# Two blocks of language-model work on one Trainium2 core: the expert stages put into one block, and the products of experts 34 to 127 widened to 512 columns

## The chip, the cores and the metric

One core of one Trainium2 chip runs the whole program. The metric is the device time of one execution in microseconds, as the median of several.

## The reference, cut to what matters

The reference runs a mixer block (attention with modulation) and then a second block on 256 tokens of width 2048, all in float32. The change lies in the last part of the second block, `peer_ffn`: 16384 small experts, of which each token and head picks 16.

```python
q = (xt @ wq).reshape(-1, PEER_HEADS, 2, PEER_HALF)          # 8 heads, 2 halves of 128
s = jnp.einsum('thpc,hpnc->thpn', q, keys)                   # 128 keys each
sv, si = lax.top_k(s, PEER_TOPK)                             # 16 best of each half
cand = (sv[:, :, 0, :, None] + sv[:, :, 1, None, :])...      # 256 sums
cid = (si[:, :, 0, :, None] * N_KEYS + si[:, :, 1, None, :])...
top_s, top_j = lax.top_k(cand, PEER_TOPK)
eid = jnp.take_along_axis(cid, top_j, axis=-1)
gate = jax.nn.softmax(top_s.astype(jnp.float32), axis=-1)
act = jax.nn.gelu(jnp.einsum('thkd,td->thk', ue, xt)...)     # ue = u[eid]
return jnp.einsum('thk,thkd->td', (gate * act).astype(xt.dtype), ve)   # ve = v[eid]
```

Then `h = layernorm(ALPHA * h + ff, ln2_g, ln2_b)`.

## The kernel before, in words

**Numbers.** Every float32 operand of a product is split into two float32r parts, hi (rounded by ScalarE) and lo (what is left, taken by VectorE). A product is three: hi hi, hi lo and lo hi, all added up in one PSUM bank (`mm3`, L159 to L164).

**Weights.** All weights go through one pipeline of slabs of 128 x 1024 values (512 KB), numbered through the whole program. SyncE loads them into four buffers `raw` (`load_slabs`, L131), ScalarE rounds halves of 512 columns into `w_hi` (`round_slab`, L146), VectorE subtracts into `w_lo` (`split_slab`, L153); both have two buffers. TensorE counts finished halves in `multiplied`, which lets ScalarE overwrite `w_hi`; `hi_ready`, `lo_ready` and `raw_ready` are the other counts.

**The expert part** computes all 16384 experts densely, 128 groups ("experts" in what follows: expert j is the row of 128 experts with first key j), and multiplies each activation with a gate that is zero where nobody picked it. It stands in three blocks, each of which ends with a barrier of all engines:

1. *Query stage* (L1612 to L1698). Transposes h, then for each of the 16 lists (8 heads, 2 halves) two slabs give a query (`query`), a small product with the keys its scores (`score`, L1641), and VectorE the 16 best (`rank`, with `top_step`). The end of the last ranking ends the block.
2. *Expert stage* (L1700 to L1863). TensorE: for expert j two slabs of `u`, 16 chunks of 128 features, three products of 256 columns (all tokens) per chunk, into bank j % 2 (`experts`, `feature_slab`). ScalarE: Gelu from PSUM into `wt[:, j, :]` (`activate`, L1752), in order with its rounding, two slabs ahead. VectorE: between the splits of the first 32 experts, for each head, the 16 best of 256 sums and the numbers of the picked experts. Then, beside experts 32 and 33, the softmax of all gates (Exp on ScalarE, L1765; the rest on VectorE, L1850 to L1853), which sets `g_ready`. GpSimd then adds the 8 x 16 x 2 columns of gates into a table in HBM, `g_dram`, by 256 indirect transfers (L1725), and waits after each head.
3. *Output stage* (L1866 to the end). GpSimd fetches the gate table, two experts at a time, through four buffers `pick` (L1891) and multiplies `wt` by them (L1896), as fast as it can, also the four last (L1912). ScalarE and VectorE split the gated weights of each expert (`wj_hi` L1922, `wj_lo` L1925) and the slabs of `v`; TensorE multiplies, 24 products of 512 columns per expert, and adds everything up in all 8 banks. A layernorm ends the program (L1963 on).

`acc_free` in stage 2 counts the banks that TensorE may write. The order on each engine is the order in which the code is written.

## Time and profile before

| what | value |
|---|---|
| time, median of 3 runs | 3189.55 us (3186.62 to 3190.53) |
| the profiled execution: its time, its span | 3186.14 us, 3184.5 us |
| granted TensorE clock, mean | 0.961 |
| TensorE, VectorE, ScalarE, GpSimd busy | 92%, 56%, 45%, 20% of the span |
| expert stage, first product to last | 1693.5 to 2432.2 us |
| output stage, first product to last | 2441.8 to 3159.6 us |
| HBM read, written | 532 MB, 21 MB: 174 GB/s |

Times on the axis of the trace count from the first instruction. "Busy" of TensorE counts overlapping products once; the length printed for one product (0.28 or 0.39 us) is its way through the array, and the pace of a full stream is the distance between starts. A bracket behind an instruction gives the idle time of its engine before it, and who ended it. In a group, busy us and the mean in ns of one stand behind the first bar, idle time before it behind the second.

### The profile page before, as it was taken

How to read it: one execution, taken by the hardware profiler on the slowest of the kernel's cores; microseconds unless marked ns; L12 is line 12 of the kernel's file. 1: busy time of each engine (PE TensorE's matmuls, PEld its weight loads, DVE VectorE, ACT ScalarE, POOL GpSimd, SP SyncE). 2: the span in 40 equal slices, each digit the busy share in tenths (PEclk: the TensorE clock that was granted, in tenths of full speed). 3: DMA queues.
4: the chain of work that ended last, by engine and by line, in shares of the span. 5: the costliest groups of instructions: out<-in, count | busy, mean ns of one | idle time of the engine just before them, and what ended most of it. 6: DMA issues, size and time to landing. Idle time of an engine off the chain costs nothing. (4 is left out here: it accounts for less than half of the span.)

```text
span 3184.5 us, 54921 instructions
## 1 busy us (share of the span) xinstructions
PE 2920.6 (92%) x17320; PEld 2551.2 (80%) x17320; DVE 1782.8 (56%) x3239; ACT 1423.2 (45%) x2600; POOL 626.3 (20%) x488
## 2 busy tenths in 40 slices
PE   6879997799989699987798999999998999999996
PEld 4658784688757599966698999999998778888885
DVE  5784325532355665446687874444445985555556
ACT  6663234422444344443344444444444445555553
POOL 0030001200000000010000028778775750000000
PEclk9999998799989799988899999999999999999998
DMA  6873237332425355534454567877777876666664
GB/s 237 288 229 127 87 111 278 93 122 96 139 85 180 99 182 188 165 126 134 162 167 154 181 185 181 182 184 180 183 184 243 278 237 193 193 192 192 194 193 132
DMA packets 182878, 554.10 MB, mean 174 GB/s; under 512 B 53664, under 2 KB 53696, under 8 KB 179488
## 3 DMA queue, kind: packets, MB, share of 16 engines
q1 hardware_dynamic: 137696, 517.03, 50.1%
q0 software_dynamic: 44544, 32.10, 6.2%
q10 hardware_dynamic: 576, 4.19, 0.3%
q8 instruction: 33, 0.54, 0.1%
q14 instruction: 29, 0.24, 0.0%
HBM read 532.13 MB, written 21.10 MB: 174 GB/s over the span
## 5 line engine op out<-in xcount | busy, mean ns | idle before, releaser
L153 DVE TENSOR_TENSOR w_lo<-raw,w_hi 128x512 fp32r<-128x512 f32 x1888 | 1319.0, 724 | 1175.8 <-ACT w_hi L146 1173.0
L146 ACT ACTIVATE w_hi<-raw 128x512 fp32r<-128x512 f32 x1888 | 1144.4, 629 | 989.9 <-PE PS L164 924.7
L162 PE MATMUL PS<-h_hi,w_hi 128*128 128x256 f32 x2944 | 833.9, 283 | 14.1 <-ACT L1753 8.6
L163 PE MATMUL PS<-h_lo,w_hi 128*128 128x256 f32 x2944 | 831.2, 282 | 0.0
L164 PE MATMUL PS<-h_hi,w_lo 128*128 128x256 f32 x2944 | 831.1, 282 | 0.0
L162 PEld LDWEIGHTS PS<-h_hi,w_hi 128*128 128x128 f32 x2944 | 564.7, 192 | 16.6 <-issue 10.9
L164 PEld LDWEIGHTS PS<-h_hi,w_lo 128*128 128x128 f32 x2944 | 564.8, 192 | 0.0
L163 PEld LDWEIGHTS PS<-h_lo,w_hi 128*128 128x128 f32 x2944 | 564.7, 192 | 0.0
L1725 POOL DMA_INDIRECT g_dram<-gt,spot x256 | 418.2, 1634 | 528.0 <-DVE gt L1853 417.9
L162 PE MATMUL PS<-w_hi,wj_hi 128*128 128x512 f32 x1024 | 402.8, 393 | 20.4 <-DVE wj_lo L1925 20.1
L164 PE MATMUL PS<-w_hi,wj_lo 128*128 128x512 f32 x1024 | 400.2, 391 | 0.0
L163 PE MATMUL PS<-w_lo,wj_hi 128*128 128x512 f32 x1024 | 400.1, 391 | 0.0
L162 PEld LDWEIGHTS PS<-w_hi,wj_hi 128*128 128x128 f32 x1024 | 193.2, 189 | 69.1 <-issue 15.2
L164 PEld LDWEIGHTS PS<-w_hi,wj_lo 128*128 128x128 f32 x1024 | 193.1, 189 | 40.6
L163 PEld LDWEIGHTS PS<-w_lo,wj_hi 128*128 128x128 f32 x1024 | 193.4, 189 | 39.8
L162 PE MATMUL PS<-x_hi,w_hi 128*128 128x256 f32 (+1 forms) x512 | 175.5, 343 | 12.1 <-ACTq L551 11.0
L1752 ACT ACTIVATE wt<-PS 128x256 f32 (+1 forms) x128 | 49.1, 384 | 298.1 <-PE PS L164 253.5
L163 PE MATMUL PS<-x_lo,w_hi 128*128 128x256 f32 (+1 forms) x512 | 174.2, 340 | 0.0
L164 PE MATMUL PS<-x_hi,w_lo 128*128 128x256 f32 (+1 forms) x512 | 174.1, 340 | 0.0
L162 PE MATMUL PS<-w_hi,x_hi 128*128 128x512 f32 x384 | 150.7, 392 | 1.3 <-DVE w_lo L153 1.3
L163 PE MATMUL PS<-w_lo,x_hi 128*128 128x512 f32 x384 | 150.3, 392 | 0.0
L164 PE MATMUL PS<-w_hi,x_lo 128*128 128x512 f32 x384 | 150.3, 391 | 0.0
(315 smaller groups left out, 2909.8 us busy)
## 6 DMA issues: line engine op xcount, KB each, us to landing
raw<-in_u_s SPq DMA_DIRECT2D x256, 512.0 KB
raw<-in_v SPq DMA_DIRECT2D x256, 512.0 KB
raw<-in_w_in_s SPq DMA_DIRECT2D x112, 512.0 KB
raw<-in_w_mod_s SPq DMA_DIRECT2D x96, 512.0 KB
raw<-in_w_in_a SPq DMA_DIRECT2D x64, 512.0 KB
raw<-in_w_in_b SPq DMA_DIRECT2D x64, 512.0 KB
raw<-in_w_out_s SPq DMA_DIRECT2D x64, 512.0 KB
g_dram<-h_buf SPq DMA_DIRECT2D x1, 16384.0 KB, 42.7
```

What stands on the lines that cost most here:

```text
L146: act.activation(w_hi[m % 2][:, half], raw[:, m % NRAW, half], ACT.Copy).then_inc(hi_ready, 1)
L153: dve.tensor_tensor(w_lo[m % 2][:, half], raw[:, m % NRAW, half], w_hi[m % 2][:, half].bitcast(F), ALU.subtract).then_inc(lo_ready, 1)
L162: pe.matmul(out, lhs[0], rhs[0], start=start, stop=False)
L163: pe.matmul(out, lhs[0], rhs[1], start=False, stop=False)
L164: return pe.matmul(out, lhs[1], rhs[0], start=False, stop=stop)
L1725: pool.indirect_dma_start(g_dram, bass.IndirectOffsetOnAxis(spot[:, t, n:n + 1], 0), gt[:, t, h, k:k + 1], None, compute_op=ALU.add).then_ ...
L1752: act.activation(wt[:, j if reg is None else reg + j, :], PS[:, j % 2, 0:T], ACT.Gelu).then_inc(acc_free, 1)
```

## The change

- The three blocks become one; nothing but counts of semaphores orders them.
- VectorE does the splits of the last two query lists inside `rank` also for slabs of `u`, and the picks of a head carry splits that lie four slabs further on. The picks run 5 heads, then `finish(0)` (softmax and places of heads 0 to 3), 3 heads, `finish(1)`.
- ScalarE does Exp in two batches (`gate_exp`), behind Gelu of expert 17 and of expert 33, and loads the Gelu table again at once. GpSimd starts to scatter heads 0 to 3 with the first batch.
- From expert 34 (`JW`) on, `h_hi` and `h_lo` lie side by side (`h_both`), and w_hi is multiplied with both in one product of 512 columns: hi hi lands in the lower half of the bank, hi lo in the upper half. w_lo times h_hi adds 256 columns to the lower half. ScalarE copies the upper half into `part`, VectorE adds the lower half (`add_low`), and ScalarE does Gelu from SBUF, one expert later.
- GpSimd fetches and weighs through two buffers (`GB` 2), four experts before the expert stage ends, and from then on at most eight experts ahead of TensorE.
- `wj_hi`, `wj_lo` lie over `si`, `spot` and `gt`; `part` lies in `pick`.

The core of the diff:

```diff
-        GB = 4
+        GB = 2
-        h_hi = buf3("h2_hi", [P, KT, T], R, hT)
-        h_lo = buf3("h2_lo", [P, KT, T], R, hT)
+        h_both = buf3("h2", [P, KT, 2, T], R, hT)
+        h_hi, h_lo = h_both[:, :, 0, :], h_both[:, :, 1, :]
...
+            part = pick[:, GB:2 * GB, :].rearrange("p a (b t) -> p (a b) t", b=2)
+            GH = HEADS // 2
+            J1 = HEADS * HEAD_SLABS // 2
+            JW = J1 + 2
...
+                    for h in range(HEADS):
+                        pool.wait_ge(g_ready, h // GH + 1)
...
+                    def weigh(reg, n):
+                        b = n // 2 % GB
+                        pool.wait_ge(gelued, max(JW, n + 2) if reg is None else reg + (n + 2))
+                        wait_multiplied(pool, None if reg is None else reg * 2, v0 + 2 * n - 16)
+                        pool.wait_ge(g_in[b], past(reg, 16 * (n // (2 * GB) + 1), 8 // GB))
+                        two = wt[:, n:n + 2, :] if reg is None else wt[:, ds(reg + n, 2), :]
+                        pool.tensor_tensor(two, two, pick[:, b, :].rearrange("p (j t) -> p j t", j=2), ALU.mult)\
+                            .then_inc(weighed, 2)
...
+                    pool.wait_ge(acc_free, JW + 2)
+                    for n in range(0, 2 * GB, 2):
+                        fetch(None, n)
+                    for n in range(0, 2 * GB, 2):
+                        weigh(None, n)
+                        pool.wait_ge(weighed, n + 2)
+                        fetch(None, n + 2 * GB)
+                    wait_multiplied(pool, None, v0)
...
+                    def experts_wide(reg, j):
+                        pe.wait_ge(acc_free, past(reg, j + 1))
...
+                                pe.matmul(PS[:, 6 + j % 2, :], w_hi[m % 2][:, c], h_both[:, kk, :, :].rearrange("p a t -> p (a t)"),
+                                          start=(kk == 0), stop=False)
+                                last = pe.matmul(PS[:, 6 + j % 2, 0:T], w_lo[m % 2][:, c], h_hi[:, kk, :],
+                                                 start=False, stop=(kk == KT - 1))
...
+                    def gate_exp(b):
+                        act.wait_ge(sh, GH * (b + 1))
+                        heads = slice(GH * b, GH * (b + 1))
+                        act.activation(gt[:, :, heads, :], gt[:, :, heads, :], ACT.Exp).then_inc(g_exp, 1)
+                        act.preload_act_table(ACT.Gelu)
...
+                    act.preload_act_table(ACT.Gelu)
+                    act.sem_inc(acc_free, 2)
+                    walk(0, J1 // 2 + 2)
+                    gate_exp(0)
+                    walk(J1 // 2 + 2, J1 + 2)
+                    gate_exp(1)
+                    def wide(reg, j):
+                        r2 = None if reg is None else reg * 2
+                        for s in range(2):
+                            round_slab(act, r2, m0 + 2 * j + s + 1)
+                        wait_multiplied(act, r2, m0 + 2 * j + 2)
+                        act.wait_ge(acc_free, past(reg, j + 1))
+                        act.activation(part[:, j % 2, :], PS[:, 6 + j % 2, T:2 * T], ACT.Copy).then_inc(low_out, 1)
+                    def gelu(reg, j):
+                        act.wait_ge(acc_free, past(reg, j + 3))
+                        act.activation(wt[:, past(reg, j), :], part[:, 2 + j % 2, :], ACT.Gelu).then_inc(gelued, 1)
+                    act.sem_inc(gelued, JW)
+                    act.wait_ge(g_ready, 2)
...
+                    with loop(act, N_KEYS - JW - 2, 2) as j:
+                        for u in range(2):
+                            wide(j, JW + 2 + u)
+                            gelu(j, JW + 1 + u)
...
+                    with loop(dve, GH + 1) as h:
+                        picks(h, 0)
+                    finish(0)
+                    with loop(dve, GH - 1) as h:
+                        picks(h, GH + 1)
+                    dve.wait_ge(tk, HEADS * per + 1)
+                    finish(1)
+                    def add_low(reg, j):
+                        dve.wait_ge(low_out, past(reg, j - JW + 1))
+                        dve.wait_ge(gelued, past(reg, j - 1))
+                        dve.tensor_tensor(part[:, 2 + j % 2, :], PS[:, 6 + j % 2, 0:T], part[:, j % 2, :], ALU.add).then_inc(acc_free, 1)
+                    with loop(dve, N_KEYS - JW, 2) as j:
+                        for u in range(2):
+                            for s in range(2):
+                                split_slab(dve, j * 2, m0 + 2 * (JW + u) + s + 1)
+                            add_low(j, JW + u)
```

Names of semaphores in the rows below are those under which they were allocated first: some carry the name of an earlier use of the same semaphore.

TensorE, from the query stage into the expert stage, before (the count it waits for at L172 is `acc_free`):

```order
L1641 MATMUL PS<-keys,qp 128x128 [waits s_free_5,acc_free_5]
L1641 MATMUL PS<-keys,qp 128x128
L64 UNCONDITIONAL_BRANCH
L1730 UNCONDITIONAL_BRANCH [waits barrier_Pool_Activation_PE_DVE_SP_release]
L34 UNCONDITIONAL_BRANCH
L34 ISA
L172 ISA [waits x_in0]
L162 MATMUL PS<-h_hi,w_hi 128x256 [waits lo_ready]
L163 MATMUL PS<-h_lo,w_hi 128x256
```

and TensorE at the start of the wide experts in the changed kernel (L1742 is the wait for a bank, L1745 the wide product, L1747 the narrow one; `h` is `h_both`):

```order
L164 MATMUL PS<-h,w_lo 128x256
L34 REGISTER_ALU
L34 COMPARE_AND_BRANCH
L34 UNCONDITIONAL_BRANCH
L34 ISA
L1742 ISA [waits x_in0]
L1745 MATMUL PS<-h,w_hi 128x512 [waits lo_ready]
L1747 MATMUL PS<-h,w_lo 128x256
```

The block's end before the experts is gone, and from expert 34 on two products stand where L162, L163 and L164 stood.

ScalarE around the softmax of the gates, before:

```order
L146 ACTIVATE w_hi<-raw 128x512 [waits multiplied,raw_ready1]
L146 ACTIVATE w_hi<-raw 128x512 [waits multiplied]
L146 ACTIVATE w_hi<-raw 128x512 [waits multiplied,raw_ready2]
L146 ACTIVATE w_hi<-raw 128x512 [waits multiplied]
L1765 ACT_TABLE_LOAD
L1765 ACTIVATE gt<-gt 128x256 [waits sh_u]
L1752 ACT_TABLE_LOAD
L1752 ACTIVATE wt<-PS 128x256 [waits multiplied]
```

and in the changed kernel at the second batch (L1813 is Gelu of a narrow expert, L1818 Exp, L1819 the load of the Gelu table, L1838 the copy of the upper half into `part`):

```order
L1813 ISA [waits multiplied]
L1813 ACTIVATE wt<-PS 128x256
L34 REGISTER_ALU
L34 COMPARE_AND_BRANCH
L1818 ACT_TABLE_LOAD
L1818 ACTIVATE gt<-gt 128x2x64 [waits sh_u]
L1819 ACT_TABLE_LOAD
L146 ACTIVATE w_hi<-raw 128x512 [waits multiplied,raw_ready1,g_ready_u]
L146 ACTIVATE w_hi<-raw 128x512 [waits multiplied]
L146 ACTIVATE w_hi<-raw 128x512 [waits multiplied,raw_ready2]
L146 ACTIVATE w_hi<-raw 128x512 [waits multiplied]
L1838 ACTIVATE pick<-PS 128x256 [waits x_in0,multiplied]
```

Two slabs were rounded ahead of Exp before; now Exp and both table loads stand ahead of the next rounding, which waits for `g_ready` too.

GpSimd, from the scatter to the weighing, before:

```order
L1725 DMA g_dram<-gt,spot 4194304x1 x31
L64 UNCONDITIONAL_BRANCH [waits scattered_u]
L1884 UNCONDITIONAL_BRANCH [waits barrier_Pool_Activation_PE_DVE_SP_gather]
L60 ISA x7
L1891 DMA pick<-g_dram 128x512 x4
L1901 DMA hb<-h_dram 128x4096 [waits h_stored]
L1903 DMA parc_12437<-in_ln_g 128x2048
L1903 DMA parc_12438<-in_ln_b 128x2048
L34 UNCONDITIONAL_BRANCH
L34 ISA
L1896 ISA [waits x_in2]
L1896 TENSOR_TENSOR wt<-wt,pick 128x512
```

and in the changed kernel (L1658 scatter, L1675 fetch, L1670 multiply, L1687 the load of h for the end):

```order
L1658 DMA g_dram<-gt,spot 4194304x1 [waits g_ready_u,scattered_u]
L1658 DMA g_dram<-gt,spot 4194304x1 x31
L1675 DMA pick<-g_dram 128x512 [waits x_in0,scattered_u]
L1675 DMA pick<-g_dram 128x512
L1670 TENSOR_TENSOR wt<-wt,pick 128x512 [waits multiplied,x_in1,normed]
L1675 DMA pick<-g_dram 128x512 [waits x_in3]
L1670 TENSOR_TENSOR wt<-wt,pick 128x512 [waits multiplied,x_in2,normed]
L1675 DMA pick<-g_dram 128x512 [waits x_in3]
L1687 DMA hb<-h_dram 128x4096 [waits h_stored,multiplied]
L1689 DMA parc_10498<-in_ln_g 128x2048
```

The block's end is gone, and each multiply waits for `multiplied`, the count of finished products, beside its fetch.

## Rows read from the trace of the kernel before

**Rows 1.** the page, section 1: busy time, share of the span and instructions of each engine

```profile
PE 2920.6 (92%) x17320; PEld 2551.2 (80%) x17320; DVE 1782.8 (56%) x3239; ACT 1423.2 (45%) x2600; POOL 626.3 (20%) x488
```

**Rows 2.** windows: length, busy us (instructions) of PE, PEld, DVE, ACT, POOL; PEclk, DMA share, GB/s

```profile
1600.00:1684.00 84.00, 84.00 (x707) 84.00 (x705) 73.22 (x302) 36.44 (x67) 0.00 (x0) 1.00 0.50 169
...
1900.00:2420.00 520.00, 520.00 (x4336) 520.00 (x4335) 233.69 (x361) 238.34 (x451) 406.85 (x250) 1.00 0.75 183
...
2470.00:2595.00 125.00, 116.75 (x494) 90.77 (x493) 113.68 (x104) 59.49 (x104) 92.11 (x97) 1.00 0.86 278
...
2640.00:3150.00 510.00, 510.00 (x2252) 422.30 (x2251) 291.49 (x470) 268.38 (x469) 0.00 (x0) 1.00 0.63 192
```

**Rows 3.** timeline of PE, query to expert stage: start, us, instruction, [idle before <-releaser]

```profile
1683.47 0.28 PE L164 MATMUL PS<-h_hi,w_lo 128*128 128x256 f32 x1
...
1693.53 0.57 PE L162 MATMUL PS<-h_hi,w_hi 128*128 128x256 f32 x1 [8.60 <-ACT L1753]
```

**Rows 4.** timeline of ACT at the same place

```profile
1683.79 0.38 ACT L1663 ACTIVATE qp<-PS 128x256 f32<-128x256 f32 x1 [2.25 <-PE PS L164]
1692.11 1.28 ACT L1753 ACT_TABLE_LOAD   x1 [7.94 <-PEq L64]
```

**Rows 5.** timeline of PE, expert stage to output stage

```profile
2432.06 0.28 PE L164 MATMUL PS<-h_hi,w_lo 128*128 128x256 f32 x1
2441.77 0.79 PE L162 MATMUL PS<-w_hi,wj_hi 128*128 128x512 f32 x1 [9.44 <-DVE wj_lo L1925]
2442.36 0.63 PE L163 MATMUL PS<-w_lo,wj_hi 128*128 128x512 f32 x1
2442.79 0.63 PE L164 MATMUL PS<-w_hi,wj_lo 128*128 128x512 f32 x1
```

**Rows 6.** timeline of ACT, expert stage to output stage

```profile
2440.73 0.42 ACT L1922 ACTIVATE wj_hi<-wt 128x256 fp32r x1 [7.87 <-POOL wt L1896]
```

**Rows 7.** timeline of DVE, expert stage to output stage

```profile
2441.29 0.42 DVE L1925 TENSOR_TENSOR wj_lo<-wt,wj_hi 128x256 fp32r<-128x256 f32 x1 [10.44 <-ACT wj_hi L1922]
```

**Rows 8.** timeline of PE, last matmul of the program

```profile
3159.41 0.39 PE L164 MATMUL PS<-w_hi,wj_lo 128*128 128x512 f32 x1
```

**Rows 9.** timeline of ACT where the gates get their exp

```profile
1882.95 1.28 ACT L1765 ACT_TABLE_LOAD   x1
1884.24 0.42 ACT L1765 ACTIVATE gt<-gt 128x256 f32<-128x256 f32 x1
```

**Rows 10.** timeline of DVE, softmax behind that exp

```profile
1884.69 0.42 DVE L1850 TENSOR_REDUCE gs<-gt 128x16 f32<-128x256 f32 x1 [1.04 <-ACT gt L1765]
...
1885.44 0.49 DVE L1853 TENSOR_TENSOR gt<-gt,gs 128x128 f32<-128x128 f32 x2
```

**Rows 11.** timeline of ACT, one expert of the expert stage

```profile
2300.00 0.38 ACT L1752 ACTIVATE wt<-PS 128x256 f32 x1 [2.35 <-PE PS L164]
2300.28 1.69 ACT L146 ACTIVATE w_hi<-raw 128x512 fp32r<-128x512 f32 x3
```

**Rows 12.** timeline of DVE, the same expert

```profile
2300.93 1.90 DVE L153 TENSOR_TENSOR w_lo<-raw,w_hi 128x512 fp32r<-128x512 f32 x3 [2.56 <-ACT w_hi L146]
```

**Rows 13.** the scatter of the gates, L1725: duration ns min/median/max, first and last start

```profile
L1725 POOL DMA_INDIRECT g_dram<-gt,spot x256: 1546/1551/2057, 1886.8 to 2413.6; - x128
```

**Rows 14.** groups by line, 2450 to 2590, while GpSimd weighs

```profile
L153 DVE TENSOR_TENSOR w_lo<-raw,w_hi 128x512 fp32r<-128x512 f32 x94 | 109.9, 1207 | 15.1 <-ACT w_hi L146 15.1
...
L1896 POOL TENSOR_TENSOR wt<-wt,pick 128x512 f32 x53 | 71.1, 1342 | 5.2 <-DMA pick<-g_dram 4.4
```

**Rows 15.** groups by line, 2640 to 3140, after it

```profile
L153 DVE TENSOR_TENSOR w_lo<-raw,w_hi 128x512 fp32r<-128x512 f32 x368 | 255.2, 693 | 214.5 <-ACT w_hi L146 214.5
```

**Rows 16.** timeline of PE near the end of the weighing

```profile
2603.01 0.49 PE L162 MATMUL PS<-w_hi,wj_hi 128*128 128x512 f32 x1 [2.43 <-DVE wj_lo L1925]
...
2604.59 0.63 PE L162 MATMUL PS<-w_hi,wj_hi 128*128 128x512 f32 x1
2605.02 0.63 PE L163 MATMUL PS<-w_lo,wj_hi 128*128 128x512 f32 x1
```

More of the change, by code:

```diff
@@ new lines, in _ @@
+                    wait_multiplied(pool, None, v0)
+                    pool.wait_ge(h_stored, 16)
+                    pool.dma_start(hb[:, :, :], h_dram).then_inc(late_in, 16)
+                    for i, name in enumerate(("ln2_g", "ln2_b")):
+                        pool.dma_start(par[i][:, :], bcast(io[name])).then_inc(late_in, 16)
+                    with loop(pool, N_KEYS - 4 * GB, 2 * GB) as j:
+                        for n in range(2 * GB, 4 * GB, 2):
+                            weigh(j, n)
+                            pool.wait_ge(weighed, j + (n + 2))
+                            fetch(j, n + 2 * GB)
@@ L1623, in _ @@
+                    for n in range(N_KEYS - 2 * GB, N_KEYS, 2):
+                        weigh(None, n)
                 @blk.tensor
@@ new lines, in _ @@
+                    expert_slab(None, v0, 0, 0, True, False)
+                    pe.wait_ge(acc_free, N_KEYS + 2)
+                    expert_slab(None, v0 + 1, 0, 1, True, False)
+                    for a in range(2):
+                        expert_slab(None, v0 + 2 + a, 1, a, False, False)
+                    with loop(pe, N_KEYS - 4, 2) as j:
+                        for u in range(2):
+                            for a in range(2):
+                                expert_slab(j, v0 + 4 + 2 * u + a, 2 + u, a, False, False)
@@ L1656, in _ @@
                     transposed_round(act, tr, h_hi, rnd, banks=(0, 1))
-                    act.sem_inc(acc_free, 2)
+                    act.sem_inc(q_free, 2)
                     with loop(act, 2 * HEADS, 2) as j:
@@ new lines, in _, with pair @@
+                    gelu(None, N_KEYS - 1)
+                    def pair(j, last):
+                        for u in range(2):
+                            split_weights(act, None, j, u)
+                            for s in range(2):
+                                if not (last and u == 1 and s == 1):
+                                    round_slab(act, None if j is None else j * 2, v0 + 2 * u + s + 1)
+                    with loop(act, N_KEYS - 2, 2) as j:
+                        pair(j, False)
@@ L1776, in _ @@
+                    dve.wait_ge(tk_q, 5 * 2 * HEADS + 1)
+                    step = chain(dve, "dve_last")
                     per = 10
```

382 lines of the change are left out of this document (154 added, 228 removed).

## The prediction

> **What bounds the kernel now.** First the page: TensorE is busy 92% of the span, VectorE 56%, ScalarE 45%, GpSimd 20% [rows 1], so most of the time can only be won by making TensorE's own stream shorter, and the rest by closing its holes. Then the windows by stage [rows 2], which tell where it is full. In the expert stage (1900 to 2420 us) PE is busy 520.00 of 520.00 us with 4336 products of 256 columns: 0.1199 us each, at granted clock 1.00, the 2.4 GHz level. An expert is 48 of them, 5.757 us. In the undisturbed output stage (2640 to 3150) it is full again: 2252 products of 512 columns in 510 us, 0.2265 us each, 24 to an expert, 5.436 us. Two 256-column products take 0.2398, so a 512-column one costs 0.0133 us less than two of 256.
>
> Between the full stretches are three holes. At the start of the expert stage the last query product begins at 1683.47, and the first expert product at 1693.53 [rows 3]: the rankings of VectorE have to end, then a block ends, then ScalarE loads a table at 1692.11 [rows 4]. At the start of the output stage the last expert product begins at 2432.06 and the first output product at 2441.77 [rows 5]: behind the block's end GpSimd must fetch and weigh before ScalarE can round the weights (2440.73) [rows 6] and VectorE take the rest (2441.29) [rows 7]. After both holes PE starts slowly, at the 1.2 GHz level: 0.43 us between 512-column products [rows 5], where 0.2265 is the rule. Third, while GpSimd weighs everything in one go (2470 to 2595), PE gets 494 products done where 125/0.2265 = 552 would fit, and VectorE is busy 113.68 of 125 us [rows 2]. The groups by line say why: w_lo<-raw,w_hi lasts 1207 ns there and 693 ns after it [rows 14, 15], beside a GpSimd multiply of 1342 ns, every 2.6 us.
>
> **The change, part by part.** All times are those of the one profiled execution (3186.14 us, span 3184.5), whose axis I carry on.
>
> *1. Query to expert stage.* No barrier is left: PE waits for acc_free, which ScalarE gives after the qp copy (1683.79) [rows 4], with its next instruction 0.28 later (as the copy at 2300.00 and its follower at 2300.28 [rows 11]), and one table load of 1.28. First expert product: 1683.79 + 0.28 + 1.28 + 0.15 for the signals = 1685.5, where it was 1693.53. That is 8.0 won. The old stage also took 2432.18 - 1693.53 = 738.65 us for 128 x 5.757 = 736.9; the 1.75 are the slow first products, and go, since PE now pauses 1.9 us with the score products in it. Against this, VectorE does its last two rankings and the first picks beside the first experts. In the query stage it is busy 73.22 of 84 us beside a full PE [rows 2], so it can just keep up; but the first split now waits for the table load, and the lag meets the first picks. I bound this stall by 0 and 3 us and take 1.5. Sum: 8.0 + 1.75 - 1.5 = **8.3 won**.
>
> *2. Gates in two batches.* Exp now stands behind the Gelu of expert 17 and of expert 33, with the next rounding behind it, where before two slabs had been rounded ahead of it. From the start of that Gelu: 0.28, Exp table 1.28 and Exp 0.4 [rows 9], Gelu table 1.28, then a half slab's rounding and, 0.65 after its start, its split of 0.69 [rows 11, 12]: 0.28 + 1.28 + 0.4 + 1.28 + 0.65 + 0.69 = 4.6 us. PE holds one prepared slab (24 x 0.1199 = 2.88), of which 0.3 has run. It waits 4.6 - 2.6 = 2.0 us. The second time ScalarE also waits for g_ready, 1.3 us of VectorE work behind Exp [rows 10], which the second table load covers. Twice 2.0: **4.0 lost** (0 if the tables did not have to change, 6 if VectorE is late as well). What it buys is an early scatter. It took from 1886.8 to 2413.6 [rows 13], 527 us; with the first batch ready near 1813 (expert 21 or 22), it ends near 2345, 60 us before the expert stage does. So fetching and weighing the first four experts costs nothing; without this lead it would be the old hole.
>
> *3. Wide products, experts 34 to 127.* Per k-chunk one 512-column and one 256-column product take the place of three: 0.2265 + 0.1199 = 0.3464 for 0.3597 us. 94 experts x 16 chunks x 0.0133 = **20.1 won**. The columns streamed are the same; what goes is the fixed part of one product in three. Above and below: the second product can't cost less than its columns do at 2.4 GHz, 0.1067, which would win 20 more; and the saving of a wide product over two narrow ones could be absent where two different weights alternate, which wins nothing. I take the row of the 512 products, where the weights also change each time. The added work is one more ScalarE activation of 0.38 and one VectorE add of about 0.42 per expert. ScalarE was busy 238 of 520 us, VectorE 234 [rows 2]. The order matters more: from the start S of the next expert, the copy starts at S+0.29, Gelu at S+0.57, rounding near S+0.92, the split ends at S+2.26, and PE wants it at S+2.77. The cover is 0.5 us, so this costs nothing; on VectorE the add lies in the gap before that split.
>
> *4. Expert to output stage.* GpSimd has weighed four experts by then. Left is the copy, Gelu of 126, the add, Gelu of 127 (start S+1.2), rounding of the weights at S+1.5, and from there to PE 2441.77 - 2440.73 = 1.04 [rows 5, 6]: 2.5 us, for 2441.77 - 2432.18 = 9.6. **7.1 won.** The fetches of h and the two parameter rows wait for the last expert product and have 690 us.
>
> *5. Weighing spread over the output stage.* The stage now lasts 3159.41 + 0.23 - 2441.77 = 717.9 us [rows 5, 8]; at full pace 128 x 5.436 = 695.8. GpSimd's multiply is now held to eight experts ahead of PE, one in 10.9 us in place of one in 2.6. A VectorE split held up for 1.3 us once in two experts has cover: a half slab is wanted 2.7 us and more after it could have been made. **22.1 won**, of which 13 are the lost products above and most of the rest the slow stretches. If each of 62 multiplies still cost what it costs now, 58 x 0.2265 / 49 = 0.27 us, 16.6 of it would stay; I take none, for the density is a quarter.
>
> *6. Clock.* A pause of 2.43 us near the end of the weighing was followed, from 2604.59, by eight products at 0.43 us [rows 16]. The pause at the switch to the output stage is nearest to it in length: I charge **1.7 lost** there, and nothing for the shorter ones.
>
> Sum: 8.3 - 4.0 + 20.1 + 7.1 + 22.1 - 1.7 = 51.9, from 3186.1 to 3134.2. The profiled execution lies 3.4 below the median of 3189.55; against the median it is 3137.7, rounded **3138 us**. Before the expert stage and behind the last product nothing changes.
>
> **Rivals.** *A, more is hidden than I see* (0.10): no stall at the gates or the start, cheaper narrow products: 5.5 and up to 10 more, 3123 to 3132. *B, the weighing still hurts* (0.08): VectorE held up by as much per multiply as now, 16.6, gives 3154. For it speaks only the 1207 ns. *C, the wide product saves nothing* (0.06): pace by columns alone, 3158. Against it stands the 0.0133 between the two full stages. The Trainium skill, page "TensorE: Matmul & The Clock Gate", section "Wait — 56ns, not 53.3ns?", has the fixed part of a product at about 2.5 ns when warm. By that rule part 3 wins 94 x 16 x 2.5 ns = 3.8 us as an estimate from the page, the sum is 3154, and the rows, with 13.3 ns, disagree.
>
> *D, slower* (0.04): the split comes late for every wide expert. ScalarE works in order, and the copy and one Gelu now stand ahead of the rounding. From a chain of 2.77 us on PE waits; from 0.55 us more per expert (51.9/94) all is lost. If Copy out of PSUM and Gelu out of SBUF had to change tables, 2 x 1.28, the chain is 4.8 and PE waits 2.05 x 94 = 193 us: 3331. Against it: Copy and Gelu alternate now, 0.28 apart, without a load [rows 11].
>
> **How the numbers follow.** My forecast has 0.72 (3132 to 3148, from the stalls at 0 to 6 and the clock at 0 to 7). The range must leave out at most 0.2: 3128 to 3156 cuts off half of A, C and D, 0.15 together. About 0.2% (6 us) is what can be told from no change. Faster 0.95, same 0.01, slower 0.04.
>
> **What would show it.** Right: wide experts 5.54 us apart with PE full; the first expert product near 1685.5; PE idle about 2 us behind L1819 twice; under 3 us before the first output product; the last scatter near 2345; w_lo near 700 to 800 ns in the output stage, and 5.44 us per expert from its beginning. Wrong: PE waiting for w_lo in the wide stretch (D), 5.7 us per wide expert (C), w_lo above 1000 ns with PE under full (B), the scatter ending behind the experts.

## The result, and the profile after

| kernel | median us | lowest to highest | ratio of the runs, 95% interval |
|---|---|---|---|
| before | 3190.04 (4 runs) | 3186.62 to 3191.83 | |
| changed | 3140.64 (4 runs) | 3137.06 to 3152.64 | 0.9853, 0.9825 to 0.9881 |

The change is 49.4 us faster, where 51.5 was forecast, and the median lies 2.6 us above the forecast of 3138. A second group of runs of the same two kernels (e1 below) has 3144.20 for 3190.49, 46.3 us; the median of all eleven executions of the changed kernel is 3142.5. The execution that was profiled took 3152.64 us (span 3150.9), 12 us more than the median of its group; the experiments below tell why.

The page of the changed kernel, section 1:

```profile
PE 2911.8 (92%) x15816; PEld 2475.9 (79%) x15816; DVE 1801.5 (57%) x3346; ACT 1450.7 (46%) x2697; POOL 621.6 (20%) x488
```

TensorE has 1504 products fewer than in [rows 1]: 94 x 16 chunks have two products in place of three. Its windows by stage (columns as in [rows 2]):

```profile
1600.00:1684.00 84.00, 84.00 (x706) 84.00 (x706) 72.59 (x298) 37.87 (x69) 0.00 (x0) 1.00 0.48 169
1900.00:2400.00 500.00, 500.00 (x2832) 433.51 (x2831) 266.09 (x442) 259.39 (x529) 353.85 (x224) 1.00 0.73 188
2450.00:2575.00 125.00, 125.00 (x553) 103.50 (x552) 79.18 (x116) 65.26 (x115) 22.31 (x24) 1.00 0.69 214
...
2640.00:3100.00 460.00, 460.00 (x2032) 380.87 (x2031) 289.21 (x424) 240.02 (x423) 73.25 (x78) 1.00 0.66 215
```

Two things stand here. In the output stage 553 products fit in 125 us, where 494 did [rows 2]: full pace from its beginning. And in the wide stretch PE is full, with 2832 products in 500 us, so a pair of them (one wide, one narrow) costs 0.3531 us, where 0.3464 was predicted.

The timeline of PE from query to expert stage answers to [rows 3]. Everything ahead runs 2.60 us later than in the profile of before (its last query product at 1686.07, there 1683.47):

```profile
1686.07 0.28 PE L164 MATMUL PS<-h,w_lo 128*128 128x256 f32 x1
1686.19 1.35 PE L1716 MATMUL PS<-keys,qp 128*128 x8
1688.21 0.38 PE L162 MATMUL PS<-h,w_hi 128*128 128x256 f32 x1 [0.68 <-ACT L1825]
```

From last query product to first expert product it is 2.14 us, for 10.06. ScalarE in front of the gates (a later stretch of its timeline) answers to [rows 9], and behind it stand the two first expert products that had to wait for the gates, on the timeline of PE:

```profile
1793.48 0.38 ACT L1813 ACTIVATE wt<-PS 128x256 f32 x1 [2.35 <-PE PS L164]
1793.88 1.28 ACT L1818 ACT_TABLE_LOAD   x1
1795.17 0.31 ACT L1818 ACTIVATE gt<-gt 128x128 f32<-128x128 f32 x1
1795.50 1.28 ACT L1819 ACT_TABLE_LOAD   x1
1796.80 2.19 ACT L146 ACTIVATE w_hi<-raw 128x512 fp32r<-128x512 f32 x4
```

```profile
1798.21 0.38 PE L162 MATMUL PS<-h,w_hi 128*128 128x256 f32 x1 [1.99 <-DVE w_lo L153]
...
1892.60 0.51 PE L1745 MATMUL PS<-h,w_hi 128*128 128x512 f32 x1 [2.04 <-DVE w_lo L153]
```

From expert to output stage PE, then VectorE and GpSimd (answering to [rows 5, 7]; the timeline of each):

```profile
2422.70 0.28 PE L1747 MATMUL PS<-h,w_lo 128*128 128x256 f32 x1
2426.52 0.80 PE L162 MATMUL PS<-w_hi,wj_hi 128*128 128x512 f32 x1 [3.53 <-DVE wj_lo L1794]
2427.11 0.63 PE L163 MATMUL PS<-w_lo,wj_hi 128*128 128x512 f32 x1
2427.54 0.63 PE L164 MATMUL PS<-w_hi,wj_lo 128*128 128x512 f32 x1
...
2445.91 0.49 PE L162 MATMUL PS<-w_hi,wj_hi 128*128 128x512 f32 x1 [1.41 <-DVE wj_lo L1794]
```

```profile
2423.53 0.42 DVE L2005 TENSOR_TENSOR pick<-PS,pick 128x256 f32<-128x256 f32 x1 [1.97 <-ACT pick L1838]
2424.90 1.56 DVE L1794 TENSOR_TENSOR wj_lo<-wt,wj_hi 128x256 fp32r<-128x256 f32 x1 [0.95 <-ACT wj_hi L1791]
```

```profile
2423.28 0.53 POOL L1687 DMA_DIRECT2D hb<-h_dram  x1 [31.82 <-PE PS L1747]
...
2424.89 1.28 POOL L1670 TENSOR_TENSOR wt<-wt,pick 128x512 f32 x1
```

The hole is 3.82 us wide, from start to start. `wj_lo`, 0.42 us as a rule, takes 1.56: GpSimd begins a multiply 0.01 us before it. The second pause, at 2445.91, comes from ScalarE, which waited for weights:

```profile
2441.24 1.22 ACT L146 ACTIVATE w_hi<-raw 128x512 fp32r<-128x512 f32 x2 [1.50 <-DMA raw<-in_v]
```

Groups by line, 2640 to 3100, answer to [rows 15]. Below them the scatter [rows 13] and PE's last product [rows 8]:

```profile
L153 DVE TENSOR_TENSOR w_lo<-raw,w_hi 128x512 fp32r<-128x512 f32 x339 | 261.2, 775 | 171.4 <-ACT w_hi L146 170.8
...
L1670 POOL TENSOR_TENSOR wt<-wt,pick 128x512 f32 x38 | 49.1, 1292 | 317.8 <-PE PS L164 317.8
```

```profile
L1658 POOL DMA_INDIRECT g_dram<-gt,spot x256: 1545/1551/3242, 1820.2 to 2342.7; - x128
```

```profile
3125.81 0.39 PE L164 MATMUL PS<-w_hi,wj_lo 128*128 128x512 f32 x1
```

### The profile page after: what moved, and what is told of

It reads as the page before. It is cut to its first block and busy times, and to the rows that moved or that the text cites. A ratio compares the mean times of both kernels' runs of the same rounds, so it can differ in the third digit from the quotient of the medians.

```text
span 3150.9 us, 52606 instructions
## 1 busy us (share of the span) xinstructions
PE 2911.8 (92%) x15816; PEld 2475.9 (79%) x15816; DVE 1801.5 (57%) x3346; ACT 1450.7 (46%) x2697; POOL 621.6 (20%) x488
## 5 line engine op out<-in xcount | busy, mean ns | idle before, releaser
L1745 PE MATMUL PS<-h,w_hi 128*128 128x512 f32 x1504 | 533.1, 400 | 2.0 <-DVE w_lo L153 2.0
L1658 POOL DMA_INDIRECT g_dram<-gt,spot x256 | 414.2, 1618 | 458.4 <-DVE gt L1986 348.7
L1747 PE MATMUL PS<-h,w_lo 128*128 128x256 f32 x1504 | 423.1, 281 | 0.0
L162 PE MATMUL PS<-w_hi,wj_hi 128*128 128x512 f32 x1024 | 399.2, 390 | 4.9 <-DVE wj_lo L1794 4.9
L163 PE MATMUL PS<-w_lo,wj_hi 128*128 128x512 f32 x1024 | 398.8, 389 | 0.0
L164 PE MATMUL PS<-w_hi,wj_lo 128*128 128x512 f32 x1024 | 398.8, 389 | 0.0
L1745 PEld LDWEIGHTS PS<-h,w_hi 128*128 128x128 f32 x1504 | 283.4, 188 | 73.2 <-DVE w_lo L153 2.4
L1747 PEld LDWEIGHTS PS<-h,w_lo 128*128 128x128 f32 x1504 | 284.8, 189 | 0.0
L162 PE MATMUL PS<-h,w_hi 128*128 128x256 f32 x800 | 228.8, 286 | 5.0 <-DVE w_lo L153 2.9
L162 PEld LDWEIGHTS PS<-w_hi,wj_hi 128*128 128x128 f32 x1024 | 192.6, 188 | 45.6 <-DVE wj_lo L1794 3.9
L163 PE MATMUL PS<-h,w_hi 128*128 128x256 f32 x800 | 227.0, 284 | 0.0
L164 PE MATMUL PS<-h,w_lo 128*128 128x256 f32 x800 | 227.0, 284 | 0.0
L163 PEld LDWEIGHTS PS<-w_lo,wj_hi 128*128 128x128 f32 x1024 | 192.6, 188 | 40.0
L164 PEld LDWEIGHTS PS<-w_hi,wj_lo 128*128 128x128 f32 x1024 | 192.5, 188 | 40.1
L1670 POOL TENSOR_TENSOR wt<-wt,pick 128x512 f32 (+1 forms) x64 | 82.7, 1292 | 533.7 <-PE PS L164 483.1
L162 PE MATMUL PS<-x_hi,w_hi 128*128 128x256 f32 (+1 forms) x512 | 175.4, 343 | 11.1 <-ACTq L551 11.0
L162 PE MATMUL PS<-h_hi,w_hi 128*128 128x256 f32 x640 | 178.1, 278 | 4.0 <-DVE w_lo L153 2.1
L163 PE MATMUL PS<-h_lo,w_hi 128*128 128x256 f32 x640 | 177.2, 277 | 0.0
L164 PE MATMUL PS<-h_hi,w_lo 128*128 128x256 f32 x640 | 177.2, 277 | 0.0
L163 PE MATMUL PS<-x_lo,w_hi 128*128 128x256 f32 (+1 forms) x512 | 174.2, 340 | 0.0
```

Source lines behind the costliest of these rows:

```text
L162: pe.matmul(out, lhs[0], rhs[0], start=start, stop=False)
L163: pe.matmul(out, lhs[0], rhs[1], start=False, stop=False)
L164: return pe.matmul(out, lhs[1], rhs[0], start=False, stop=stop)
L1658: pool.indirect_dma_start(g_dram, bass.IndirectOffsetOnAxis(spot[:, t, h, k:k + 1], 0), gt[:, t, h, k:k + 1], None, compute_op=ALU.add).th ...
L1670: pool.tensor_tensor(two, two, pick[:, b, :].rearrange("p (j t) -> p j t", j=2), ALU.mult)\
L1745: pe.matmul(PS[:, 6 + j % 2, :], w_hi[m % 2][:, c], h_both[:, kk, :, :].rearrange("p a t -> p (a t)"), start=(kk == 0), stop=False)
```

## The measure of the experiments

Each profiled execution was one of the runs of its row, and the rest of a row have a time alone. The first transposition of the query stage starts anywhere between 1567.92 and 1583.69 us in the fourteen profiles, though the program up to there is the same. So two lengths are read from each profile: **X**, from that start to the start of the last expert product, and **Y**, from there to the start of the last product of the program. X holds parts 1 to 3 of the prediction, Y parts 4 to 6. Where the same work was measured again at the same pace, X agrees within 0.1 us (e1, e4 and e11; e6, e7 and e12; before, e8 and e10). Y of the changed kernel is 702.07 to 703.11.

| profile | wide products in 400 us of the wide stretch | X | Y | median us (runs) |
|---|---|---|---|---|
| before | none | 858.89 | 727.35 | 3190.04 (4) |
| changed | 2266 | 846.94 | 703.11 | 3140.64 (4) |
| e1_again, the same | 2309 | 836.98 | 702.80 | 3144.20 (6) |
| e11_third, the same | 2310 | 836.91 | 702.07 | 3133.78 (1) |
| e2_narrow | none | 856.79 | 699.85 | 3159.16 (6) |
| e3_grouped | 2283 | 843.13 | 701.51 | 3151.88 (5) |
| e4_h_late | 2309 | 836.98 | 706.30 | 3148.09 (5) |
| e5_burst | 2266 | 846.98 | 705.77 | 3153.41 (4) |
| e6_gate_ahead | 2266 | 840.83 | 703.09 | 3141.77 (5) |
| e7_both | 2266 | 840.78 | 700.41 | 3142.87 (4) |
| e12_both2, as e7 | 2266 | 840.81 | 700.40 | 3141.82 (4) |
| e8_before_spread | none | 858.89 | 709.27 | 3166.66 (6) |
| e10_before_two | none | 858.88 | 715.16 | 3171.17 (6) |
| e9_two_two | 2298 | 833.27 | 700.51 | 3139.39 (4) |

The count is of both products of the pairs, 1900 to 2300 (e3: 1920 to 2320, since its second gate pause reaches past 1900). Before ran beside each group of experiments: 3190.49 (e1 to e4), 3187.74 (e5 to e8), 3186.14 (e9 to e12).

## The experiments

**e1_again and e11_third: the changed kernel twice more.** No edit.

> The changed kernel once more, for a second profile. If the pace of the wide experts is a property of the program, 16 pairs of a 512- and a 256-column product again take 5.65 us (0.3531 us per pair, as in the first profile) and the time is near 3140. If it was an accident of that one execution, which was 12 us above the median of the other three, the pair takes about 0.346 us and the profiled time is 3137 to 3142.

> The changed kernel a third time, for the pace of its wide experts alone. If the pace differs from execution to execution (0.3531 us per pair in the first profile, 0.3465 in the second), this shows one of the two, and from the first transposition to the last output product it takes 1539.8 (fast pace) or 1550.0 us (slow), within 1.5 us. A third value would speak against two states.

The same program ran its wide stretch at two paces. Windows of the changed kernel, of e1 and of e11:

```profile
1900.00:2300.00 400.00, 400.00 (x2266) 346.75 (x2265) 212.29 (x353) 207.79 (x425) 313.95 (x197) 1.00 0.74 186
```

```profile
1900.00:2300.00 400.00, 400.00 (x2309) 352.69 (x2309) 218.25 (x362) 212.31 (x434) 313.49 (x197) 1.00 0.77 189
```

```profile
1900.00:2300.00 400.00, 400.00 (x2310) 352.69 (x2309) 217.71 (x360) 211.80 (x433) 310.45 (x193) 1.00 0.77 189
```

0.3531 us a pair in the first, 0.3465 in the others; full both times, at granted clock 1.00. 1504 pairs times 0.0066 are 9.9 us, and X differs by 10.0. So the pace holds for the whole wide stretch, and the time from X's start to Y's end, 1539.8 (e1) and 1539.0 us (e11), fits what was expected for the fast pace. It accounts for 10 of the 12 us that the first profile lies above the median, though the pace of the three runs without a profile is not known.

**e2_narrow: the wide products undone.** Experts 34 to 127 get their three 256-column products back, and Gelu reads PSUM again (so GpSimd counts `acc_free` in place of `gelued`); all else stays.

```diff
-                        pool.wait_ge(gelued, max(JW, n + 2) if reg is None else reg + (n + 2))
+                        pool.wait_ge(acc_free, max(JW, n + 2) + 2 if reg is None else reg + (n + 4))
...
-                            experts_wide(j, JW + u)
+                            experts(j, JW + u)
...
-                    wide(None, JW)
...
-                    gelu(None, N_KEYS - 1)
+                    walk(JW, N_KEYS)
...
-                            add_low(j, JW + u)
```

> One block, batched gates and the spread weighing kept, experts 34 to 127 with three 256-column products as before, Gelu straight from PSUM. Theory: the wide products alone win 94 x 16 x (0.3597 - 0.3531) = 10 us, so this is 10 us slower than the changed kernel, about 3150. My prediction's term says 20 us, 3160. Rival, that the wide products win nothing, says the same time as the changed kernel, 3140.

In X the wide products are worth 856.79 - 836.98 = 19.8 us at 0.3465 and 9.85 at 0.3531. But Y is 2.2 to 3.3 us shorter in e2 (699.85): without the copy, the add and the second Gelu `wj_lo` (from 2433.30 us, 0.42 long) is done when the multiply begins at 2433.72, the hole at the switch is 2.24 us and no slow products (0.43 us in place of 0.2265) follow it. So the wide products win 16.9 to 17.7 us in X and Y together at the fast pace and 6.6 at the slow one; the medians differ by 15.0. What remains of X against before, 2.1 us, is parts 1 and 2 together.

**e3_grouped: four wide products, then four narrow ones.**

```diff
-                                last = pe.matmul(PS[:, 6 + j % 2, 0:T], w_lo[m % 2][:, c], h_hi[:, kk, :],
-                                                 start=False, stop=(kk == KT - 1))
                                 if k % 4 == 3:
+                                    for q in range(k - 3, k + 1):
+                                        c = slice(q * P, (q + 1) * P)
+                                        kk = 8 * half + q
+                                        last = pe.matmul(PS[:, 6 + j % 2, 0:T], w_lo[m % 2][:, c], h_hi[:, kk, :],
+                                                         start=False, stop=(kk == KT - 1))
```

> The same products, but in each half slab the four 512-column ones first and then the four 256-column ones. If it is the change of length from product to product that costs, four and four take 4 x 0.2265 + 4 x 0.1199 = 1.386 us for the 1.412 of now: a wide expert 5.54 to 5.56 us, 8 to 10 us faster than the changed kernel. If a product after h_both or w_lo is slower by itself, the pace stays at 5.65 us and the time the same.

```profile
1920.00:2320.00 400.00, 400.00 (x2283) 349.55 (x2282) 214.51 (x356) 209.05 (x426) 311.42 (x198) 1.00 0.76 187
```

A third value, 0.3504, between the two, and not the 8 to 10 us that were expected: the median is 7.7 us above that of e1. Alternating two sizes of product is not what costs the 0.0066 us: with the same alternation one program ran at 0.3531 and at 0.3465, and a quarter of the changes of size gave, in this one profile, no better pace.

**e4_h_late: the fetch of h and of the two parameter rows moved to the end of the weighing.**

```diff
-                    wait_multiplied(pool, None, v0)
-                    pool.wait_ge(h_stored, 16)
-                    pool.dma_start(hb[:, :, :], h_dram).then_inc(late_in, 16)
...
                             fetch(j, n + 2 * GB)
+                    wait_multiplied(pool, None, v0)
+                    pool.wait_ge(h_stored, 16)
+                    pool.dma_start(hb[:, :, :], h_dram).then_inc(late_in, 16)
```

> The loads of h and of the two parameter rows (4 MB) are moved from the start of the output stage to near its end. Theory: they crowd out slab loads and a fetch, so PE's wait of 1.8 us some 20 us into the output stage goes (it followed a rounding that waited for raw<-in_v), and the first multiply no longer starts beside the first wj_lo (1.56 us in place of 0.42), since the multiplies of experts 4 to 7 come before the stage: the pause before the first output product falls from 3.8 to about 2.6 us. Together 3 to 5 us faster, with the slow products behind the pause. Rival: the pause is the chain of copy, add, Gelu and rounding alone, and the time stays within 1 us.

The hole at the switch shrinks to 2.68 us, as expected, and no pause follows within the next 30 us. But two pauses come where the fetch now is, the longer with seven products at 0.43 us behind it (timeline of PE, then of ACT):

```profile
3048.64 0.49 PE L162 MATMUL PS<-w_hi,wj_hi 128*128 128x512 f32 x1 [1.06 <-DVE wj_lo L1794]
...
3056.90 0.49 PE L162 MATMUL PS<-w_hi,wj_hi 128*128 128x512 f32 x1 [2.47 <-DVE wj_lo L1794]
```

```profile
3050.00 1.15 ACT L146 ACTIVATE w_hi<-raw 128x512 fp32r<-128x512 f32 x2 [2.32 <-DMA raw<-in_v]
3053.40 1.15 ACT L146 ACTIVATE w_hi<-raw 128x512 fp32r<-128x512 f32 x2 [2.25 <-DMA raw<-in_v]
```

Y is 3.5 us longer than that of e1, where 3 to 5 us less was expected for the whole: this expectation missed. Held against the same load at the start of the stage, the cost isn't a fixed one: the pause of 1.79 us from start to start in the changed kernel's first profile was 0.79 in e11, and in e1 there was none and no wait of ScalarE for a slab.

**e5_burst: the hold of eight experts taken out of the weighing.**

```diff
-                        wait_multiplied(pool, None if reg is None else reg * 2, v0 + 2 * n - 16)
```

> The changed kernel with GpSimd's wait for TensorE's progress taken out of the weighing, so that it multiplies as fast as two buffers and its fetches allow. Theory (the density of the multiplies costs, not their number): w_lo<-raw,w_hi goes from 775 ns to 1000 to 1200 ns over the first 160 to 200 us of the output stage, PE is not full there, and the program is 10 to 20 us slower than the changed kernel, about 3158. Rival (a multiply costs the same wherever it stands): the time stays within 3 us of 3144.

10 to 20 us were expected. Profile against profile at the same pace 2.7 came (Y 705.77 for 703.11). The medians lie further apart, 3153.41 against 3144.20 and 3140.64. The slow pace of the pair, which this profile has and some of the other executions have not, may account for 10 us of that, but for the runs without a profile that isn't shown. The groups and the window while it weighs, 2460 to 2580, tell why Y lost little:

```profile
L153 DVE TENSOR_TENSOR w_lo<-raw,w_hi 128x512 fp32r<-128x512 f32 x88 | 80.1, 923 | 31.6 <-ACT w_hi L146 31.5
...
L1669 POOL TENSOR_TENSOR wt<-wt,pick 128x512 f32 x33 | 46.6, 1411 | 34.2 <-DMA pick<-g_dram 34.0
```

```profile
2460.00:2580.00 120.00, 119.00 (x522) 97.31 (x521) 89.09 (x110) 61.70 (x109) 64.41 (x66) 1.00 0.84 262
```

With two buffers in place of four GpSimd waits for its fetches (34.2 us) and multiplies once in 120/33 = 3.6 us, not in 2.6. `w_lo` takes 923 ns, where 1000 to 1200 were expected, and that is thin enough: 522 products where an unhindered stage has 531 (the changed kernel, same window).

**e8_before_spread and e10_before_two: each half of part 5 alone, in the kernel before.** e8 has the hold and keeps four buffers; e10 has two buffers and no hold.

```diff
                     def weigh(reg, b):
+                        wait_multiplied(pool, reg * 2, m0 + 4 * b - 16)
...
                         n = N_KEYS - 2 * GB + 2 * b
+                        wait_multiplied(pool, None, m0 + 2 * n - 16)
```

```diff
-        GB = 4
+        GB = 2
         pick_at = nc.sbuf_base
-        pick = buf3("pick", [P, GB, 2 * T])
+        pick = buf3("pick", [P, 4, 2 * T])
...
-                        pool.wait_ge(g_in[b], 16 if reg is None else reg * 2 + 16)
+                        pool.wait_ge(g_in[b], 16 if reg is None else reg * 4 + 16)
```

> The kernel before with one thing of the change alone: each multiply of the weighing waits until TensorE is within eight experts. Theory: 15 to 18 us faster than the kernel before, about 3173, with PE at 0.2267 us per product from soon after the start of the output stage; the 9.6 us ahead of the stage stay. Rival: most of the 22 us that the output stage won in the changed kernel came with the removal of the barrier, and this wins under 5 us.

> The kernel before with one thing changed: GpSimd fetches through two buffers in place of four, with no wait for TensorE. In the run with the burst the two buffers alone held the multiplies 4.3 us apart, and PE lost about 2 us. Theory (density decides, from somewhere between one in 4.3 and one in 2.6 us): the output stage loses 3 to 6 us in place of 22, so this is 13 to 18 us faster than the kernel before, about 3173. Rival: in the program with barriers the multiplies hurt whatever their distance: under 5 us.

The window 2460 to 2580 of before, of e8 and of e10:

```profile
2460.00:2580.00 120.00, 112.57 (x477) 87.83 (x476) 108.29 (x100) 56.47 (x99) 88.37 (x94) 1.00 0.86 278
```

```profile
2460.00:2580.00 120.00, 120.00 (x532) 99.37 (x531) 75.72 (x111) 63.02 (x111) 20.45 (x22) 1.00 0.72 217
```

```profile
2460.00:2580.00 120.00, 118.81 (x520) 96.84 (x519) 87.00 (x109) 61.92 (x109) 59.60 (x60) 1.00 0.83 256
```

The hold alone wins 727.35 - 709.27 = 18.1 us of Y, the two buffers alone 12.2. X is untouched by both. The medians, against those of before in the same groups, say 21.1 and 15.0. e8 was expected to win 15 to 18 us, e10 13 to 18: by Y the first is met and the second 0.8 short, by the medians the first is 3 over and the second met. Both rivals, under 5 us, fall. The hole at the switch stays in e8 (10.02 us), and 18.1 plus the 6.2 by which the changed kernel narrows it are the 24.2 that Y won. So the hold by itself, without the new order of the stages, gives all that part 5 gave. In the changed kernel, which has the two buffers as well, taking the hold out loses 2.7 of it (e5): either of the two thins the multiplies.

**e6_gate_ahead, e7_both, e12_both2: the gates behind two rounded slabs, then also the late loads in parts.** In e6 ScalarE rounds both slabs of the next expert, does Exp, and only then Gelu; e7 and e12 (the same kernel) fetch h and the two rows as four parts of 1 MB, 24 experts apart.

```diff
+                    def gated(j, b):
+                        for s in range(2):
+                            round_slab(act, None, m0 + 2 * j + s + 1)
+                        gate_exp(b)
+                        wait_multiplied(act, None, m0 + 2 * j + 2)
+                        act.activation(wt[:, j, :], PS[:, 6 + j % 2, 0:T], ACT.Gelu).then_inc(acc_free, 1)
```

```diff
+                        if i < 2:
+                            pool.dma_start(hb[:, i, :], h_dram[:, i, :]).then_inc(late_in, 16)
...
+                    for i in range(5):
+                        at = 2 * GB + 24 * i
...
+                        late(i)
```

> Exp of both gate batches stands behind the rounding of two slabs and ahead of the Gelu of experts 17 and 33, as before the change, in place of behind those Gelus. Theory: the two pauses of PE of 2.28 us between starts behind the gates go, and with them some of the slow products after the second: 4 to 5 us faster than the changed kernel, about 3139. Rival: the pause is hidden elsewhere or moves to the next slab, and the time does not change. In the profile the pair of the wide experts takes 0.3465 or 0.3531 us; if a pause ahead of the stream is what leads to the slow pace, it is 0.3465 here.

> The gates as in the run before, and h and the parameter rows loaded in four parts of 1 MB, each 24 experts apart, from expert 28 of the output stage on. Theory: no DMA wait of ScalarE 15 us into the output stage or later, no multiply beside the first wj_lo: 3 to 4 us more, about 3136, and PE without a gap from its first output product to its last. Rival: each 1 MB still delays a slab by more than the four buffers cover, PE has four short gaps, and nothing is won.

> The version of e7_both once more. Its profile had the slow pace, and took 1541.2 us from the first transposition to the last output product. With the slow pace again it takes 1541.2, with the fast one 1531.3, within 1.5 us. Against the changed kernel at the same pace it is 8.8 us faster; the medians, 3142 and 3141 to 3144 so far, can't tell it.

Both gate pauses are gone. Groups of PE in the expert stage, of the changed kernel and of e6:

```profile
L1745 PE MATMUL PS<-h,w_hi 128*128 128x512 f32 x1504 | 533.1, 400 | 2.0 <-DVE w_lo L153 2.0
...
L162 PE MATMUL PS<-h,w_hi 128*128 128x256 f32 x540 | 153.0, 283 | 2.9 <-DVE w_lo L153 2.9
```

```profile
L1745 PE MATMUL PS<-h,w_hi 128*128 128x512 f32 x1504 | 531.5, 399 | 0.0
...
L162 PE MATMUL PS<-h,w_hi 128*128 128x256 f32 x526 | 149.0, 283 | 0.9 <-DVE w_lo L153 0.9
```

X is 846.94 - 840.83 = 6.1 us shorter, both at 0.3531, and Y of e7 and e12 is 2.7 shorter than that of e6: the hole at the switch is 2.68 us (`wj_lo` back to 0.43), and behind it stand seven or eight slow products but no second pause. GpSimd's multiply (at 2417.62 us in e7) now stands ahead of `wj_lo` and beside the last add, which it leaves at 0.42 us. 4 to 5 us were expected of the gates and 3 to 4 of the loads. X + Y of e12 is 1541.2 us, as expected for the slow pace. In the medians, 3141.8 to 3142.9, none of these 8.8 us shows. All three profiles ran at 0.3531, the changed kernel in two of three at 0.3465. If the runs without a profile are divided likewise, that hides it; it isn't shown. Whether the gate order has to do with the pace, or it fell so, is not settled. That a pause ahead of the wide stretch is what leads to the slow pace is refuted: without them it came three times. (The counts of the 256-column products differ by where the windows begin.)

**e9_two_two: e7 with two wide products, then two narrow ones.**

```diff
+                                wide_one(k)
+                                if k % 2:
+                                    narrow_one(k - 1)
+                                    last = narrow_one(k)
```

> The best version so far (gates behind the rounding, h and parameter rows in four parts), with the wide experts' products in the order wide, wide, narrow, narrow. Wide and narrow one by one gave a pair 0.3465 us in two profiles and 0.3531 us in five (one by one) or one (four and four, 0.3527). Theory A: the pace is a state that the stream falls into at its start, whatever the order: 0.3465 or 0.3531 again, time 3133 to 3145. Theory B: the order decides, and two and two has a pace of its own, as 2 x 0.2289 + 2 x 0.1200 = 0.698 us for two pairs.

```profile
1900.00:2300.00 400.00, 400.00 (x2298) 349.00 (x2297) 216.37 (x359) 208.60 (x431) 314.81 (x201) 1.00 0.77 189
```

0.3481 us a pair, 0.696 for two, and X is 7.5 us shorter than that of e7 (1504 x 0.0050 = 7.5). It is neither of the two values of Theory A and lies by the 0.698 of Theory B; but it is one profile, and a pace has differed between executions before. (In the recorded text, the 0.3527 of four and four is from 1900 to 2300, which holds the end of a pause, and 0.3531 had been seen in four profiles by then, not five.) With X + Y = 1533.8, where the changed kernel has 1539.0 to 1550.1, this is the best version by X + Y. Its median, 3139.39 (3136.24 to 3140.24), lies 1.3 us below that of the changed kernel, which these runs can't tell from nothing.

## Why the prediction was right, and where it was off

The chain of the argument held: all three holes were where the rows put them, each narrowed by the part that was to do it, and rivals B and D did not come. The nearness of the number, 2.6 us, is in part luck. Against the 51.9 of the sum, X + Y won 36.2 in the first profile and 46.5 and 47.3 in its repeats: at no pace as much as forecast.

1. **Query to expert stage, 8.3 predicted, 8.0 measured.** From the first transposition to the first expert product it takes 112.45 us, where it took 120.36, and the next 16 experts take 0.1 less. The first expert product came 2.14 us behind the last query product (predicted 2.03). The first splits cost one pause of 1.21 from start to start, about 1.1 lost, where 1.5 was taken; the slow first products of before were 1.4 by their starts, not 1.75.
2. **Gates, 4.0 lost predicted, 6.1 measured.** The pauses, 1.99 and 2.04, are right to 0.05 us, and the early scatter that they buy ended at 2342.7 (2345 predicted). Mis-sized was what follows: step 6 charged nothing for a slow start behind pauses as short as these, but in each of the seven profiles with both pauses PE ran slowly behind one of them, and lost about 1.6 us by it. Behind which one differs: the changed kernel, behind the first and the second pause, then e11, the same program, at the same places (mean granted clock 1.00, 0.79, 0.79, 1.00):

```profile
1798.00:1806.00 8.00, 7.79 (x65) 7.79 (x66) 7.63 (x24) 3.59 (x7) 0.00 (x0) 1.00 0.46 173
1892.00:1900.00 8.00, 7.40 (x33) 6.37 (x34) 4.58 (x8) 3.44 (x7) 6.61 (x5) 0.79 0.57 132
```

```profile
1790.00:1798.00 8.00, 7.59 (x51) 7.59 (x52) 6.29 (x18) 3.22 (x8) 0.00 (x0) 0.79 0.44 131
1886.00:1894.00 8.00, 7.71 (x44) 6.81 (x45) 5.05 (x9) 3.76 (x8) 6.78 (x5) 1.00 0.72 170
```

3. **Wide products, 20.1 predicted.** 19.8 at a pace of 0.3465, 9.85 at 0.3531. The price of 0.3464 was one of the values that the pair takes, not the only one. Rival C, no gain, fell; so does the rule of the Trainium skill, page "TensorE: Matmul & The Clock Gate", section "Wait — 56ns, not 53.3ns?", whose fixed part of about 2.5 ns would have won 3.8 us, as an estimate from the page. Not in the sum was what the added copy and add cost at the switch, 2.2 to 3.3 us of Y (e2).
4. **Expert to output stage, 7.1 predicted, 5.9 measured.** The hole is 3.82 us from start to start, where the sum gives 2.6. Missed was that the same event, the end of the last expert product, releases GpSimd's multiply, which begins beside `wj_lo` and makes it 1.14 us longer. Without that collision it is 2.68 (e4, e7), so the chain itself was right.
5. **Weighing, 22.1 predicted, 18.1 measured.** That is the hold alone (e8), and the stage runs at full pace with `w_lo` at 775 ns, as was to be seen. Of the 22.1 some 2.7 were the slow start behind the hole, which a hold does not take away: e8 still has it.
6. **Clock, 1.7 lost predicted.** Slow products behind the switch lose 1.5 us in the first profile (2426.52 to 2429.58) and in e11, and 2.9 in e1, where they are twice as many. Not in the sum was the pause of 1.79 from start to start at 2445.91: "have 690 us" was true of when h is needed, and silent on what 4 MB at once can do to the slabs (1.79, 0.79 and no pause in the three profiles). Parts 4 to 6 together: 27.5 predicted, 24.2 to 25.3 measured.

So the forecast of the time was nearer than its terms: parts 4 to 6 were forecast 2.2 to 3.3 us too high, the loss at the gates 2.1 too low, and both errors point the same way. Single executions differ by 10 us in the pace of the pair and by up to 16 in their start; the forecast knew of neither, and the medians (49.4 and 46.3 us) came out nearer to it than X + Y.

## What to carry to other kernels

Cost everything that an event releases, not only the engine that you are watching: what is let go in the same moment meets (here `wj_lo` and a multiply). A burst on a helper engine is cheap when dealt out in small parts. A large load beside a steady stream is safer so: in one piece it cost PE from nothing (e1) to over 5 us, slow products included (e4), in four parts no pause in three profiles (e7, e9, e12), though ScalarE waited 1.33 and 1.43 us for a slab once in e9 and e12. Measure a stage from one of its own marks to another before you compare medians: here a start that wanders by 16 us, and a pace that differs between executions by 10, cover what a step is worth. And take more than one profile before you explain a pause: the same pause was followed by slow products in one execution and not in the next.

## What the runs showed of the hardware that was not expected

**A product's pace takes a few steps.** Full streams of 256-column products run at 0.1199 (before, narrow experts, 3336 in 400 us; 0.1200 from start to start), but another stage of before has this:

```profile
1240.00:1290.00 50.00, 50.00 (x444) 50.00 (x443) 24.51 (x39) 24.16 (x47) 0.00 (x0) 1.00 0.59 190
```

That is 0.1133 us from start to start (a short window counts a product or two too many at its edges), and the same window in e2, e3 and e9, whose program is the same up to there, has 427, 0.1178 from start to start; the other eleven profiles have the first value. 512-column products take 0.2267 in every output stage and 0.2333 at 660 to 730 in all fourteen. The pair took 0.3531, 0.3504, 0.3481 and 0.3465, each through the whole wide stretch, the granted clock being 1.00 in each of these windows. What sets the step was not found: not the alternation of sizes alone (one program had two values), not a pause ahead of it (e6).

**GpSimd's multiply costs by its density.** In the changed kernel, from 2300 us on, a VectorE split `w_lo` takes 693 ns when no multiply runs beside it (536 of them, up to 694) and 1350 ns on average when one does (62 of them). The means of a stretch are mixtures of the two: 693 ns without multiplies [rows 15], 775 with one in about 11 us, 923 with one in 3.6, 1207 with one in 2.6 [rows 14]. PE lost nothing at the first, 9 products of 531 at the second and 54 at the third. The Trainium skill, page "SBUF — State Buffer", section "SBUF: two separate sides", has a VectorE instruction with two inputs in SBUF and a GpSimd one that reads SBUF share a pair of ports, which the first one locks for its whole instruction. The rows agree (`wj_lo` 1.56 us beside a multiply of 1.28, 0.42 alone). The add, which reads one input from PSUM, stays at 424 to 425 ns beside a multiply (five cases in e7), and ScalarE's rounding at 633 ns (631 without one). The runs show besides that what the lock costs PE hangs on the time that VectorE has to spare between two multiplies.

**A slow start is not a matter of the pause's length alone.** Behind the first gate pause (1.99 to 2.00 us idle) fourteen products were slow in e2, e5 and e11 and at most one in the changed kernel, e1, e3 and e4; behind the second (1.99 to 2.06 idle) it was the other way round, with nine to eleven. Behind 1.97 idle at the switch in e2 no product was slow, behind 2.39 to 2.40 in e4, e7, e9 and e12 seven or eight were, behind 3.52 to 3.53 six or seven in four profiles and thirteen in two (e1, e6), behind 9.44 to 9.74 twelve. They take 0.43 us for 512 columns and 0.21 for 256, the pace of the 1.2 GHz level.
